# Attention products of a two-stage transformer kernel: fp32 matmuls replaced by three fp32r products, each block worked part by part

## What is computed

```python
for i in range(DEPTH):                       # 2 layers
    x = layer_norm(a * x + 0.5 * swiglu_ffn(x, ffn_w_in[i, 0], ffn_w_out[i, 0]), ...)
    if m == 0:                               # layer 0
        h = diff_attention(x, da_w_qkv[j], da_w_o[j], ...)
    elif m == 1:                             # layer 1
        h = pool_mixer(x, ...)
    x = layer_norm(a * x + h, ...)
    x = layer_norm(a * x + memory_cross_attention(x, mem, xa_wq[i], xa_wkv[i], xa_wo[i]), ...)
    x = layer_norm(a * x + 0.5 * swiglu_ffn(x, ffn_w_in[i, 1], ffn_w_out[i, 1]), ...)
```

## Time and profile before

| | |
|---|---|
| median of 3 runs | 2807.39 us (2800.92 to 2808.79) |
| the profiled execution | 2806.97 us, its span 2805.2 us |
| PE matmul busy | 2563.5 us, 91% of the span |
| DVE, ACT busy | 1371.6 us (49%), 401.0 us (14%) |
| mean granted TensorE clock | 0.959 of full |
| 0 to 1090 us | first model (PE busy nearly throughout, DMA mostly half used) |
| from about 1400 us | most of it the experts, where the DMA runs at up to 422 GB/s |

### The profile page before, as it was taken

How to read it: one execution, slowest core, us unless ns; L and a number is a source line. 1 busy time by engine, 2 the same in 40 slices (tenths; PEclk the granted TensorE clock), 3 DMA queues, 4 the chain that set the end, 5 groups by cost and what they waited for, 6 DMA issues and landing times.

```text
span 2805.2 us, 35678 instructions
## 1 busy us (share of the span) xinstructions
PE 2563.5 (91%) x13990; PEld 1632.2 (58%) x13990; DVE 1371.6 (49%) x2351; ACT 401.0 (14%) x861; POOL 62.5 (2%) x108
## 2 busy tenths in 40 slices
PE   7999999999999999997999969999998997777776
PEld 6994566799899677993555423333333773323233
DVE  6764431577777538765777833322325343211113
ACT  0000312100100121001111011111110432111111
POOL 1000000000000010000000000000000000000000
PEclk9999999999999999998999979999999998888988
DMA  7568532355555744565212369999998417999997
GB/s 262 191 228 317 207 105 98 102 180 180 181 190 193 271 174 164 192 228 170 60 60 105 142 266 422 422 422 422 422 422 352 181 39 320 422 422 422 421 422 310
DMA packets 233307, 709.06 MB, mean 253 GB/s; under 512 B 12581, under 2 KB 134453, under 8 KB 177792
## 3 DMA queue, kind: packets, MB, share of 16 engines
q1 hardware_dynamic: 223328, 676.37, 62.5%
q0 software_dynamic: 9312, 30.06, 3.1%
q10 hardware_dynamic: 576, 1.35, 0.1%
HBM read 706.59 MB, written 1.15 MB: 252 GB/s over the span
## 4 chain that ended last, share of the span: by engine, by line
PE 59%; DMA 23%; issue 11%; DVE 5%; ACT 1%; SPq 1%; POOL 0%; ACTq 0%; DVEq 0%; POOLq 0%
PE work L825 43%; PE acc L825 14%; DMA ring<-in_moe_down 13%; DMA ring<-in_moe_up 8%; PE work L841 2%; DMA ring<-in_ffn_w_in 1%; DMA ring<-in_ada_w 1%; SPq L685 1%; ACT cols_x L1561 0%; DVE stats L2052 0%; DVE rows_x L2031 0%; DVE rows_h L2069 0%; DVE stats L2018 0%; DMA rows_x<-in_x 0%; DVE rows_x L2012 0%
## 5 line engine op out<-in xcount | busy, mean ns | idle before, releaser
L825 PE MATMUL work<-ring,scratch 128*64 128x512 f32 (+1 forms) x3008 | 556.9, 643 | 107.1 <-DMA ring<-in_moe_up 61.7
L825 PE MATMUL work<-rows_h_parts,ring_parts 128*128 128x256 f32 x2816 | 517.7, 284 | 14.7 <-DVE cols_x_parts L1984 12.8
L825 PEld LDWEIGHTS work<-rows_h_parts,ring_parts 128*128 128x128 f32 x2816 | 445.3, 193 | 17.7 <-issue 12.7
L825 PEld LDWEIGHTS work<-ring,scratch 128*64 128x64 f32 (+1 forms) x3008 | 145.7, 126 | 494.2 <-issue 277.9
L825 PE MATMUL work<-cols_x_parts,ring_parts 128*128 128x256 f32 x1408 | 400.3, 284 | 0.0
L1922 DVE TENSOR_TENSOR ring_parts<-ring,ring_parts 128x2048 fp32r<-128x2048 f32 x132 | 302.5, 2292 | 4.5
L825 PE MATMUL work<-cols_x,ring 128*128 128x256 f32 (+1 forms) x896 | 282.0, 475 | 6.2 <-DVE ring L2286 2.9
L825 PEld LDWEIGHTS work<-cols_x_parts,ring_parts 128*128 128x128 f32 x1408 | 272.2, 193 | 1.4
L825 PEld LDWEIGHTS work<-cols_x,ring 128*128 128x128 f32 x896 | 169.9, 191 | 114.3 <-issue 101.3
L825 PE MATMUL acc<-ring_parts,rows_h_parts 128*128 128x512 f32 x704 | 218.0, 391 | 0.0
L825 PE MATMUL work<-scratch 128*128 128x256 f32 (+4 forms) x1040 | 200.2, 380 | 6.4 <-issue 4.2
(11 more groups left out here) (263 smaller groups left out, 2339.1 us busy)
## 6 DMA issues: line engine op xcount, KB each, us to landing
ring<-in_moe_down SPq DMA_DIRECT2D x128, 1024.0 KB, 25.9
ring<-in_moe_up SPq DMA_DIRECT2D x127, 1024.0 KB, 26.3
ring<-in_moe_gate SPq DMA_DIRECT2D x121, 1024.0 KB, 25.1
ring<-in_ffn_w_in SPq DMA_DIRECT2D x88, 1024.0 KB, 6.4
ring<-in_ada_w SPq DMA_DIRECT2D x48, 1024.0 KB, 10.5
ring<-in_ffn_w_out SPq DMA_DIRECT2D x44, 1024.0 KB, 6.7
ring<-in_xa_wkv SPq DMA_DIRECT2D x16, 1024.0 KB, 7.3
ring<-in_da_w_qkv SPq DMA_DIRECT2D x12, 1024.0 KB, 14.3
```

The lines of the kernel that those rows point to most:

```text
L825: ins = nc.tensor.matmul(o, lhsT, rhs, start=start, stop=stop, **kw)
```

## The change

The products da_qkv, da_out, xa_q and xa_out of both layers become split products, with their weight loads taking two ring slots each (load in the even, high part in the odd). For these loads ACT makes the high part (`weight_high`) and DVE the low part (`weight_low`). PE no longer alternates the three products matmul by matmul: within a block it does all high x high, then x_low x w_high, then x_high x w_low, each group behind its own semaphore. The first block of every FFN is likewise ordered high x high, w_low x x_high, w_high x x_low, and PE enters an FFN when `x_high` is there. DVE splits one FFN load ahead of the norm in place of two, and the second behind the low parts of x. The two memsets of the padded queries move from ahead of the rope to column block 4. The context norm is written to the first two tiles of `rows_h`, since `x_high` fills the other two.

```diff
+HIGH_STAGES = ("x_cols", "ffn_norm0", "da_cols", "mix_norm0", "xa_cols0", "xa_norm0", "ffn_norm1", "mix_norm1", "xa_cols1",
+               "xa_norm1")
-        plan.add(f"xa_q{i}", loads=4, tiles=4)
+        plan.add(f"xa_q{i}", loads=8, splits=4, tiles=4)
-        plan.add(f"xa_out{i}", loads=4, acc=1)
+        plan.add(f"xa_out{i}", loads=8, splits=4, acc=1)
-    plan.add("da_qkv", loads=12, tiles=12)
+    plan.add("da_qkv", loads=24, splits=12, tiles=12)
-    plan.add("da_out", loads=4, acc=1)
+    plan.add("da_out", loads=8, splits=4, acc=1)
...
 PE
+            SPLIT_ORDER = ((0, 0), (0, 1), (1, 0))
+            def rows_out_split(stage, xs, x_stage):
+                at = plan[stage]
+                for cb in range(6):
+                    t = at.tiles + NT * cb
+                    outs = [open_tile(t + j) for j in range(NT)]
+                    for half in range(2):
+                        b = 2 * cb + half
+                        n = at.loads + 2 * b
+                        weight_high_done(n)
+                        ws = parts(n, 4)
+                        for wp, xp in SPLIT_ORDER:
+                            if wp:
+                                split_done(stage, b)
+                            for j in range(NT):
+                                if b == 0 and not wp and not xp:
+                                    high_done(x_stage, j)
+                                elif b == 0 and xp:
+                                    for piece in range(2):
+                                        read_out(pe, col_tile(x_stage, j, piece))
+                                c = slice(j * P, (j + 1) * P)
+                                for k in range(4):
...
+            def cols_out_split(stage, xs, x_stage):
...
+            def out_product_split(stage, x_stage):
...
+                                if it is None and u == 0 and h == 0 and a == 0:
+                                    for wp, xp in ((0, 0), (1, 0), (0, 1)):
+                                        if xp:
+                                            for j in range(NT):
+                                                for piece in range(2):
+                                                    read_out(pe, col_tile(source, j, piece))
...
                 for j in range(NT):
-                    for piece in range(2):
-                        read_out(pe, col_tile(source, j, piece))
+                    high_done(source, j)
...
-                all_read(t)
...
 ACT
+            def weight_high(stage, k):
+                n = plan[stage].loads + 2 * k
+                act.wait_ge(load_landed[n % RING], 16 * (n // RING + 1))
+                act.wait_ge(loads_used, n + 2)
+                nc.scalar.activation(ring_parts[:, (n + 1) % RING, :], ring[:, n % RING, :],
+                                     ACT.Copy).then_inc(load_landed[(n + 1) % RING], 16)
             def cross_attention(i):
-                norm(f"mix_norm{i}", rooted=NT)
+                weight_high(f"xa_q{i}", 0)
+                for j in range(NT):
+                    split_cols(f"mix_norm{i}", j)
                 at = plan[f"xa_q{i}"]
+                for k in range(1, 3):
+                    weight_high(f"xa_q{i}", k)
...
-                rows_to_cols(f"xa_cols{i}")
+                for j in range(NT):
+                    split_tiles(plan[f"xa_cols{i}"].tiles + 2 * j, j)
+                for k in range(2, 4):
+                    weight_high(f"xa_out{i}", k)
...
-            norm("ffn_norm0", rooted=NT, between=[memory_cols])
+            split_cols("ffn_norm0", 0, da_x_high)
+            memory_cols()
+            weight_high("da_qkv", 0)
+            split_cols("ffn_norm0", 1, da_x_high)
+            for k in range(1, 12):
+                weight_high("da_qkv", k)
...
 DVE
+            def weight_low(stage, k):
+                n = plan[stage].loads + 2 * k
+                dve.wait_ge(load_landed[(n + 1) % RING], 16 * ((n + 1) // RING + 1))
+                nc.vector.tensor_tensor(ring_parts[:, n % RING, :], ring[:, n % RING, :],
+                                        ring_parts[:, (n + 1) % RING, :].bitcast(F32), ALU.subtract).then_inc(split_ready, 1)
...
-                split_first(i, 2)
+                split_first(i, 1)
...
+                    cols_low(col_tile(source, j, 0), j)
+                split_first(i, 2)
...
             def cross_attention(i):
+                for j in range(NT):
+                    cols_low(col_tile(f"mix_norm{i}", j, 0), j)
+                for k in range(4):
+                    weight_low(f"xa_q{i}", k)
+                for k in range(2):
+                    weight_low(f"xa_out{i}", k)
                 attention(f"xa_att{i}", XA_H, xa_begin, xa_weigh, XA_DK)
+                for j in range(NT):
+                    cols_low(plan[f"xa_cols{i}"].tiles + 2 * j, j)
+                for k in range(2, 4):
+                    weight_low(f"xa_out{i}", k)
                 if i == 1:
                     dve.wait_ge(ctx_landed, 16)
-                    mod_norm("ctx_norm", [1])
-                split_first(2 * i + 1, 2)
+                    mod_norm("ctx_norm", [1], dst=lambda i: rows_h[:, i - NT, :])
+                split_first(2 * i + 1, 1)
```

More of the change, by code:

```diff
@@ new lines, in cols_out_split @@
+            def cols_out_split(stage, xs, x_stage):
+                at = plan[stage]
+                for cb in range(4):
+                    t, n = at.tiles + cb, at.loads + 2 * cb
+                    weight_high_done(n)
+                    ws = parts(n, KB)
+                    o = open_tile(t).rearrange("p (a t) -> p a t", a=2)
+                    for a in range(2):
+                        c = slice(a * P, (a + 1) * P)
+                        for wp, xp in SPLIT_ORDER:
+                            if wp:
+                                split_done(stage, cb)
+                            elif cb == 0 and a == 0:
+                                for j in range(NT):
+                                    if xp:
+                                        for piece in range(2):
+                                            read_out(pe, col_tile(x_stage, j, piece))
+                                    else:
+                                        high_done(x_stage, j)
+                            for k in range(KB):
+                                fin = bool(wp and k == KB - 1)
+                                mm(o[:, a, :], ws[wp][:, k, c], xs[xp][:, k, :], k == 0 and not wp and not xp, fin,
+                                   tile_full[t % 4] if fin and a else None, done=2 * int(fin and a))
@@ L1080, in cross_attention @@
             def cross_attention(i):
[L1082 removed]
+                normed_to_cols(f"mix_norm{i}", read=False)
                 q = plan[f"xa_q{i}"]
[L1084 removed]
+                cols_out_split(f"xa_q{i}", (x_high, x_low), f"mix_norm{i}")
                 for b in range(4):
@@ L1405, in _ @@
             ada(0)
-            normed_to_cols("ffn_norm0", between=[memory_cols])
+            normed_to_cols("ffn_norm0", between=[memory_cols], read=False)
             all_read(plan["mem_cols"].tiles)
             at = plan["da_qkv"]
-            rows_out(at.loads, at.tiles, cols_x, 6)
+            rows_out_split("da_qkv", (da_x_high, x_low), "ffn_norm0")
             t = plan["da_turn"].tiles
@@ L1767, in _ @@
             for b in range(4):
+                weight_high("da_out", b)
                 memory_keys(0, b)
-            rows_to_cols("da_cols")
+            for j in range(NT):
+                split_tiles(plan["da_cols"].tiles + 2 * j, j)
             for j in range(NT):
@@ L2566, in _ @@
                 .then_inc(heads_normed, 1)
+            for k in range(4):
+                weight_low("da_out", k)
+            for j in range(NT):
+                cols_low(plan["da_cols"].tiles + 2 * j, j)
             layer_norm("mix_norm0", "da_out", ALPHA, LN_EPS)
```

109 lines of the change are left out of this document (84 added, 25 removed).

## The result

The changed kernel takes 2773.97 us (median of 4 runs, 2771.08 to 2777.10), the kernel before on the same chips 2805.87 (2800.92 to 2808.79). The ratio is 0.9889, with a 95% interval of 0.9875 to 0.9903: faster by 31.9 us, or 1.1%. The forecast was 2771.5, within 2763 to 2785. The profiled execution took 2774.7 us with a span of 2772.6; the span before was 2805.2. So the two traces differ by 32.6 us, where the sum said 35.4.

A forecast was written before the change was run, and what follows sets the result against it. PE held 59% of the chain, DMA 23%, so PE's product cost came first. Terms 17.2 + 2 x 6.9 + 2 x 2.1 + 2.0 + 0.2 - 2.0 = 35.4 us off 2806.97 gave 2771.5 us, range 2763 to 2785.

The forecast's parts named there:

- da_qkv: Stage da_qkv: 17.2 us net gain, block 0 waiting 0.5 but starting 0.6 earlier, later blocks not held up.
- PE's work: All changed products: three-part products at 0.227 us per 128x512 matmul save 43.7 us of PE work.
- da_out and xa_out0: These two stages: 5.7 us less PE work plus 1.2 us less waiting for ACT's copies, 6.9 us each.
- the quarter: Rival for PE's products: each part costs a quarter of true fp32, saving 11.5 us more, 2760 us; chance 0.03.
- The casts: Weight loads' parts: a high part takes 1.9 us on ACT, a low part 2.29 us on DVE.
- the bound in da_qkv: Rival: DVE's cover of 1.9 us per column block fails in da_qkv, 10.5 us back, 2782 us; chance 0.08.
- ffn0: Start of ffn0: PE starts near 14, idles some 7 us for the same load; clock fall taken as 2.0 us loss.
- xa_q0, xa_q1: Both stages: 4.7 us less PE work, less 1.6 for a later start and 1.0 for the low part: 2.1 each.
- the clock rival: Rival: waits at ffn0, xa_q0, xa_q1 and ahead of ffn3 cost 3 us each by slower clock, 2781 us; chance 0.06.
- xa_out1: From attention's end to ffn3: DVE is the bound, so the gain is 2.0 us, not 6.9.
- ffn1 and ffn2: Starts of these FFNs: nothing at ffn1, where PE arrives last; 0.2 us gain at ffn2.
- The second model: The experts' stretch: length unchanged, with the gain made ahead of it carried through to the end.

The follow-up runs named there:

- The version with ACT's early cast and the memory first: Changed kernel with memory tiles turned ahead of x's first tile and ACT casting da_qkv's first load between the norm's two roots: 2770.53 us, ratio 0.9874.
- the left-out matmuls: Changed kernel with 24 of the 32 matmuls of the weights' low part left out in each of xa_out0 and xa_out1: 2771.30 us, ratio 0.9872.
- the repeated run: The changed kernel measured a second time without any edit: 2773.15 us, ratio 0.9881 to the kernel before.

## Why the prediction was right, and where not

- **PE's work** was right to the hundredth: 5.44 us for 24 matmuls in da_qkv, 6.9 us each in da_out and xa_out0. The Trainium skill, "FP8 and Floating Point Precision", section "TensorE Precision Notes", gives true fp32 four passes through the array. An estimate by a quarter of the fp32 time for each part would have made a block 24 x 0.215 = 5.16 us; the trace has 5.44, so the quarter does not hold here, and why is open.
- **The casts**: 1.92 us on ACT for a forecast of 1.9, 2.29 on DVE as said. DVE did not become the bound in da_qkv: no wait for L2068 in the later blocks.
- **da_qkv is the step that failed.** "DVE ... is free for the low parts of x" and "block 0 waits 0.5 and starts 0.6 earlier: nothing net" left out who releases the PSUM tiles. With ada's shift of 1.7 the forecast start is 226.2; PE started at 230.26, 4.1 late, and its first 16 matmuls took 5.93 us where 16 x 0.227 = 3.63 are full pace. 4.1 + 2.3 less the 0.5 in the sum is 5.9, the whole difference of 17.2 and 11.3. The version with ACT's early cast and the memory first got it all back, so the tile's release is shown as the cause of the late start. How much the clock adds is partly chance: with the like wait ahead of the same turns, the version with ffn0's old entry took 3.81 us for the first sixteen matmuls, not 5.93.
- **xa_q0, xa_q1**: start and late low part as priced, each for 2.1. xa_q0 gave 0.9, since the clock fell behind its waits (0.58 and 0.56 granted between 436 and 440); xa_q1, with the like waits, kept it and gave 1.7. In four versions with the same order of work there it was the other way round (46.4 to 46.6 us for xa_q0, 46.7 to 47.1 for xa_q1), so which of the two loses more is not set by the order of work. Of the four places of the clock rival, this one cost about 1 us more than the sum had, not 3; but the clock also fell at da_qkv, where the rival had no place. What the prediction held against the rival, that waits near 1 us left the clock at full, was true of its one trace only: in the repeated trace of the kernel before it fell behind such waits.
- **xa_out1**: 2.1 for 2.0, and the left-out matmuls show that the bound is DVE's.
- **ffn0**: -1.7 for -2.0, by the mechanism given; the old entry is 0.9 to 2.6 us better. **ffn1 and ffn2** together: 0.1 for 0.2.
- **The second model** was to be unchanged. With the same code it took 1542.4 and 1538.3 us in two traces of the kernel before, and 1535.5 to 1540.6 in eleven traces of the kernels with the change. The 4.2 us of the first comparison are within this scatter. The medians put the whole gain at 31.9 and, beside the repeated run, 33.4 us, against 28.4 and 29.6 of the first model's traces. Whether 2 or 3 us of the second model are real stays open.

## What to carry to other kernels

When an operation gets a second reader on another engine, ask first which buffer that reader now releases, and what stands ahead of it in its queue. "The consumer may start on the first half" is true only if the output buffers are free too. Place casts where their engine is idle ahead of the data; here such moves, the tile order and the old entry of ffn0 were worth 18 us together, more than half of what the change itself brought.

## What the runs showed beyond that

The granted clock, not the wait alone, made the price of short stalls. In the changed kernel's trace the 3.16 us of waiting ahead of 225.61 were followed by a start 4.1 us late and 2.3 us lost in pace. And the same waits can leave the clock full or halve it. Ahead of the second modulation PE has three waits of 0.50 to 0.66 us in every version. In the changed kernel the clock stayed full; in the version with xa_q's casts early, whose work up to there is the same, it fell (first the changed kernel, then that version):

```profile
299.00:303.00 4.00, 2.69 (x20) 1.00 1.10 348
303.00:307.00 4.00, 3.52 (x32) 1.00 1.03 295
```

```profile
298.00:302.00 4.00, 2.34 (x16) 1.00 1.09 348
302.00:306.00 4.00, 3.88 (x20) 0.57 0.88 263
```

Five of the versions, this one among them, show one or two such falls between da_qkv and the keys' end, with 82.3 to 84.0 us instead of 81.0. A stage may thus change by 3 us in a trace without an edit to it, which is more than several terms of the sum.
